# A hybrid decoder layer on one core: gate tiles of the delta rule end at slots 4 and 12, the recurrence's second gate products come one step later, and decode sums, loads and first tiles are moved

## What is computed

```python
def hybrid_layer(x, lw, dn_s0, dn_buf0, lru_h0, lru_buf0, mem_k, mem_v, fox_attend):
    h = rms_norm(x, lw['norm_w'])
    proj = jnp.einsum('bsd,de->bse', h, lw['w_in']) + lw['b_in']
    (dn_qkv, dn_z, dn_b, dn_a, lru_x, lru_g, fq, fk, fv, ff, fg, mq, mg, mgate) = jnp.split(proj, IN_OFFSETS, axis=-1)
    qkv, dn_buf = causal_conv(dn_qkv, dn_buf0, lw['dn_conv_w'])
    qkv = jax.nn.silu(qkv)
...
    o, dn_s = gated_delta_rule(q, k, v, beta, log_alpha, dn_s0)
...
...
    o = fox_attend(fq, fk, fv, logf)
    out_c = (o.reshape(bn, s, BR_WIDTH) * jax.nn.silu(fg)).astype(x.dtype)
...
    o = mem_attend(mq, mem_k, mem_v)
    out_m = (o.reshape(bn, s, BR_WIDTH) * jax.nn.silu(mg)).astype(x.dtype)
    branches = jnp.stack([out_a, out_b, out_c, out_m], axis=2)
    up = jnp.einsum('bsnw,nwd->bsnd', branches, lw['w_branch'])
    gates = jax.nn.sigmoid(mgate.reshape(bn, s, N_BRANCH, D_MODEL))
    merged = jnp.sum(gates * up, axis=2)
    y = x + jnp.einsum('bsd,de->bse', merged, lw['w_out'])
```

## Time and profile before

| | |
|---|---|
| median of 3 runs | 1766.01 us (1761.44 to 1767.62) |
| profiled execution | 1764.75 us, its span 1763.1 us |
| PE busy | 1677.8 us, 95% of the span |
| DVE busy | 789.7 us, 45% |
| ACT busy | 533.0 us, 30% |
| POOL busy | 513.8 us, 29% |
| DMA | 163.21 MB, mean 93 GB/s |

### The profile page before, as it was taken

How to read it: one execution, slowest core, us unless ns; L and a number is a source line. 1 busy time by engine, 2 the same in 40 slices (tenths; PEclk the granted TensorE clock), 3 DMA queues, 4 the chain that set the end, 5 groups by cost and what they waited for, 6 DMA issues and landing times. The chain is left out here.

```text
span 1763.1 us, 26818 instructions
## 1 busy us (share of the span) xinstructions
PE 1677.8 (95%) x11027; PEld 1603.1 (91%) x11027; DVE 789.7 (45%) x1200; ACT 533.0 (30%) x895; POOL 513.8 (29%) x387
## 2 busy tenths in 40 slices
PE   5999989999999999889999999999999989999999
PEld 5899989999999999889889898999989988899976
DVE  5485753333333334650365511344667431734611
ACT  6222343222222222233234323321145213544300
POOL 1343316333334314611344331112211211012300
PEclk9999999999999999999999999999999999999999
DMA  4211154222222116423365342145210322433531
GB/s 136 50 42 46 49 153 114 67 67 67 65 56 67 49 49 174 143 73 96 92 173 158 108 132 88 51 132 150 66 36 25 112 81 84 136 96 118 154 91 55
DMA packets 189366, 163.21 MB, mean 93 GB/s; under 512 B 18380, under 2 KB 157055, under 8 KB 188726
## 3 DMA queue, kind: packets, MB, share of 16 engines
q1 hardware_dynamic: 189246, 161.51, 31.7%
HBM read 131.38 MB, written 30.22 MB: 92 GB/s over the span
## 5 line engine op out<-in xcount | busy, mean ns | idle before, releaser
L275 POOL TENSOR_TENSOR wL<-w_raw,wH 128x1024 fp32r<-128x1024 f32 (+1 forms) x113 | 245.7, 2174 | 860.4 <-ACT wH L268 860.3
L299 PE MATMUL ps<-hH,wH 128*128 128x344 f32 x1920 | 448.1, 342 | 20.7 <-PEq L195 7.7
L299 PE MATMUL ps<-hL,wH 128*128 128x344 f32 x1920 | 410.2, 322 | 0.0
L299 PE MATMUL ps<-hH,wL 128*128 128x344 f32 x1920 | 409.1, 322 | 0.0
L299 PEld LDWEIGHTS ps<-hH,wH 128*128 128x128 f32 x1920 | 314.2, 191 | 34.1 <-issue 23.9
L299 PEld LDWEIGHTS ps<-hL,wH 128*128 128x128 f32 x1920 | 326.5, 190 | 0.0
L299 PEld LDWEIGHTS ps<-hH,wL 128*128 128x128 f32 x1920 | 324.3, 190 | 0.0
L268 ACT ACTIVATE wH<-w_raw 128x1024 fp32r<-128x1024 f32 (+1 forms) x116 | 108.4, 934 | 112.9 <-PE ps L299 96.1
L2776 POOL TENSOR_SCALAR fa_logits<-fox_c_bc,token_scalars 128x128 f32<-128x128 f32 (+7 forms) x32 | 56.3, 1758 | 68.7 <-PE ps L2801 50.5
L2919 DVE SCALAR_TENSOR_TENSOR fa_logits<-ps,fox_rq,fa_logits 128x512 f32<-128x512 f32 (+3 forms) x48 | 28.2, 613 | 106.8 <-POOL fa_logits L2777 56.8
L1757 ACT ACTIVATE d_m<-ps 128x512 f32<-128x512 f32 x48 | 28.6, 595 | 141.9 <-PE ps L1933 141.9
(11 more groups left out here) (560 smaller groups left out, 2820.5 us busy)
## 6 DMA issues: line engine op xcount, KB each, us to landing
w_raw<-in_w_in SPq DMA_DIRECT2D x80, 512.0 KB, 5.3
m_th<-gate_spill SPq DMA_DIRECT2D x28, 516.0 KB, 4.5
gate_spill<-d_gate SPq DMA_DIRECT2D x18, 516.0 KB, 3.0
fa_kv<-in_cache_fox_k SPq DMA_DIRECT2D x32, 256.0 KB, 3.1
fa_kv<-in_cache_fox_v SPq DMA_DIRECT2D x32, 256.0 KB, 3.2
w_raw<-in_w_branch SPq DMA_DIRECT2D x32, 256.0 KB, 2.7
gate_spill<-fa_gate SPq DMA_DIRECT2D x10, 516.0 KB
x_rows<-in_x_prompt SPq DMA_DIRECT2D x8, 512.0 KB, 6.2
```

Of the source, the lines that this page charges most:

```text
L275: pool.tensor_tensor(self.wL[:, t % 2, 0:nk], self.raw_at(t)[:, 0:nk], self.wH[:, t % 2, 0:nk].bitcast(F32), ALU.subtract).then_inc(self.w ...
L299: last = pe.matmul(self.ps[:, b + g, 0:cols], w[:, t % 2, k], x[:, k, g * cols:(g + 1) * cols], start=(k == 0 and n == 0), stop=(k == nk - ...
```

## The change

Parts, in the order of the program. Names are those of the diff.

- **A, setup.** x_sample is loaded first, weights 1 to 3 earlier. `first_tiles` (`two_tiles`) runs column group 0 (344 columns, from x rows 0 to 3) of tiles 0 and 1 first, while the second half of h is made, and then groups 1 and 2 of both. One of the nine row blocks is scaled on POOL. The small columns come two tiles later.
- **B, dn_z.** DVE splits the second memory tile's low part ahead of the last silu product, not after.
- **C, delta rule.** `FIRST = 11`: 11 steps of gate tiles run before chunk 0, so that tiles end at slots 4 and 12; ACT empties them at slots 5 and 13 and splits weights at 6 and 14. POOL's `identity` and the late weights' split come ahead of the Gram part of the chunk after.
- **D, fk.** The weights of tile end + 2 are loaded ahead of the eight stores of the decode states.
- **E and I, fq and mq.** `ahead` and `project_alone`: tile 0 of fq and of mq runs before the barrier, and the row turns beside these tiles come one tile later.
- **F, attend.** The sums of the decode values are made by DVE: a product in place over NP x 512, for fox a sum of halves, then a sum into QB or DLG; PE only adds over the partitions by one 128x1 matmul with ones, two iterations later. KEYS, VALUES and the softmax's places are tables, denser for fox and later for the memory. LEAD and NORMS are 6 and 4 for both.
- **G and L, after attend.** The last two turns of the output (`owed`) run ahead of steps 1 and 4 of the next tile.
- **H, lru.** `k -= j`: the products of tile j come j steps later, the tail at step 2 of tile 2.

```diff
-    def project_step(self, pe, t, xH, xL, k, groups=3, cols=G3):
+    def project_step(self, pe, t, xH, xL, k, groups=3, cols=G3, only=None):
...
+    def project_alone(self, t):
+        @self.block.tensor
+        def _(pe):
+            self.project(pe, t, self.hH, self.hL)
+    def project(self, pe, t, xH, xL, groups=3, cols=G3, meanwhile=None):
+        owed, self.owed = self.owed, {}
         for k in range(self.tiles[t][1]):
-            if ahead:
-                ahead(k)
+            if k in owed:
+                owed[k](pe)
...
+        def two_tiles(pe):
+            for k in range(KD):
+                pe.wait_ge(lo, k + 1)
+                K.project_step(pe, 0, K.hH, K.hL, k, only=(0,))
+                if k < 2:
+                    turn(pe, 6 + k)
+                if k == 4:
+                    pe.wait_ge(by_act, 1)
+                    pe.wait_ge(by_dve, 6)
+                    pe.wait_ge(by_pool, 1)
+                if k >= 4:
+                    turn(pe, 4 + k)
+            for k in range(KD):
+                K.project_step(pe, 1, K.hH, K.hL, k, only=(0,))
...
+            pe.wait_ge(sample, 3)
+            for k in range(KD):
+                pe.wait_ge(lo, KD + k + 1)
+                K.project_step(pe, 0, K.hH, K.hL, k, only=(1, 2))
+            for k in range(KD):
+                K.project_step(pe, 1, K.hH, K.hL, k, only=(1, 2))
...
+                    if j == 3 and next_by_dve:
+                        dve.wait_ge(K.w_lo, K.at_lo)
+                        K.split_lo(dve, t0 + 4 + 2)
...
+        FIRST = 11
...
+                        if s == 5:
+                            gate(mid(ch))
+                        if s == 13:
+                            gate(late(ch))
...
-                        bulk(tile_of(ch, s), s % 8)
+                        q = FIRST + SLOTS * ch + s
+                        bulk(t0 + q // KD, q % KD)
...
-        if (j, k) == (2, 0):
+        if (j, k) == (2, 2):
             pe.wait_ge(N["gate"], 24)
             self.tail.pe(pe, 0)
+        k -= j
...
                 if side:
+                    K.loads(sp, end + 3)
                     side.sync_last(sp)
...
-    LEAD, NORMS = (6, 4) if fox else (3, 2)
+    LEAD, NORMS = 6, 4
...
+    if fox:
+        KEYS, LOGF, MAX, EXP, TURN, LAST = (3, 4, 5, 6, 7, 11, 12, 13), 14, 15, 16, 17, 31
+        VALUES = (19, 20, 21, 22, 23, 27, 28, 29)
+    else:
+        KEYS, LOGF, MAX, EXP, TURN, LAST = (4, 6, 8, 10, 12, 14, 16, 18), 19, 19, 20, 21, 31
+        VALUES = (22, 23, 24, 25, 26, 27, 28, 29)
...
-                    for g in range(NP):
-                        last = pe.matmul(BANK[:, r:r + 1], KV[:, b % 2, g, h], PC[:, g, r:r + 1],
-                                         start=(g == 0), stop=(g == NP - 1))
+                    last = pe.matmul(BANK[:, r:r + 1], SUMS[b % 2][:, h], K.ones[:], start=True, stop=True)
...
-                turn_back(len(its) - 2)
-                turn_back(len(its) - 1)
+                K.owed = {1: lambda pe: turn_back(len(its) - 2), 4: lambda pe: turn_back(len(its) - 1)}
...
+                def decode_values(b):
...
+                    v.do(dve.tensor_tensor(kv, kv, PC[:, :, b * H:(b + 1) * H].unsqueeze(3).broadcast_to(
+                        [P, NP, H, P]), ALU.mult))
+                    if NP == 4:
+                        v.do(dve.tensor_tensor(kv[:, 0:2], kv[:, 0:2], kv[:, 2:4], ALU.add))
...
+                    dve.tensor_tensor(SUMS[b % 2], kv[:, 0], kv[:, 1], ALU.add).then_inc(M["vs"], 1)
```

More of the change, by code:

```diff
@@ L399, in _ @@
             act.wait_ge(filled, 1)
-            for t in range(9):
+            for x, t in enumerate((TT8, 0, 1, 2, 3, 4, 5, 6, 7)):
                 n = P if t < TT8 else NB
@@ L415, in _ @@
             act.activation(K.hH[:, :, SEQ:TOK], HS[:], ACT.Identity).then_inc(sample, 1)
-            for x in range(5, 10):
+            for x in range(11, len(TURNS)):
                 high(x)
-            K.split_hi(act, 2)
-            for x in range(10, len(TURNS)):
-                high(x)
+            K.split_hi(act, 3)
             act.wait_ge(tabT, 1)
@@ L471, in turn @@
             g, k = TURNS[x]
-            if x >= 5:
-                pe.wait_ge(lo, x - 4)
+            if held(x) is not None:
+                pe.wait_ge(lo, held(x) + 1)
             for y, t in enumerate(GROUPS[g]):
@@ L492, in _ @@
             pe.wait_ge(by_dve, 4)
[L493 to L501 removed]
+            for x in range(6):
                 turn(pe, x)
@@ L773, in _ @@
                                        bias=K.bias[:, b:b + 1]).then_inc(K.evac_act, 1)
-                    if small and j == 0:
+                    if small and j == 2:
                         small.act_split(act)
@@ L830, in _ @@
             def _(pe):
-                for j in range(n):
-                    if small and j == 3:
+                if first_tiles:
+                    first_tiles(pe)
+                for j in range(2 if first_tiles else 0, n):
+                    if small and j == 5:
                         pe.wait_ge(small.N["z"], 1)
                     K.project(pe, t0 + j, K.hH, K.hL,
-                              meanwhile=small and (lambda k, j=j: small.pe_step(pe, j, k)),
-                              ahead=ready and j == 0 and (lambda k: ready(pe, k)))
+                              meanwhile=small and (lambda k, j=j: small.pe_step(pe, j, k)))
                     if 3 <= j < squares + 3:
@@ L1094, in sync @@
                 each(sp, d)
-        K.loads(sp, self.end + 2)
+        K.loads(sp, self.end + (3 if self.ahead else 2))
         if self.fetch:
@@ L1182, in _ @@
             def _(pool):
-                m.pool(pool, m.end + 1)
+                m.pool(pool, m.end + (2 if m.ahead else 1))
             @block.scalar
@@ L1187, in _ @@
                 m.act(act, m.end + 1)
+                if m.ahead:
+                    K.split_hi(act, m.end + 2)
             @block.vector
@@ L2008, in _ @@
                         turn(0)
+                for q in range(KD, FIRST):
+                    bulk(t0 + q // KD, q % KD)
                 for ch in range(NCH):
@@ L2424, in _ @@
                 if side:
+                    K.loads(sp, end + 3)
                     side.sync_last(sp)
+                if ahead:
+                    K.loads(sp, end + 3)
                 if settle:
@@ L2441, in _ @@
                     K.split_lo(pool, end + 1 if preload else end)
+                if ahead:
+                    K.split_lo(pool, end + 2)
             @block.scalar
@@ L2470, in _ @@
                         act.activation(SQ[:, j % 2], DST[:, j, 0:SEQ], ACT.Square).then_inc(sq, 1)
+                if ahead:
+                    K.split_hi(act, end + 2)
                 if late:
@@ L2477, in _ @@
                     pe.wait_ge(*first)
-                for j in range(n):
+                for j in range(1 if begun else 0, n):
                     todo = of(j)
@@ L3209, in build @@
                 project_tiles(K, at["fv"], 4, BROW["fv"], VX, "fv", turns=turns,
-                              rows=(k_rows, sizes, K.knw, after), late=decode, ready=K.emptied(at["fv"] - 1), turned_first=True,
+                              rows=(k_rows, sizes, K.knw, after), late=decode, ready=K.emptied(at["fv"] - 1), turned_first=True, ahead=True,
                               stores=[((turns.normed, j + 1), d, k_rows[j])
                                       for j, d in enumerate(rows_of("fox_k", "fox_k_s"))])
+            K.project_alone(at["fq"])
         with K.joined():
@@ L3216, in build @@
             turns = RowTurns(K, "fvr")
-            after = [turns.out(j // 3, VX[:, :, cols(j)], v_rows[j], n) for j, n in enumerate(sizes)]
+            after = [turns.out(1 + j // 3, VX[:, :, cols(j)], v_rows[j], n) for j, n in enumerate(sizes)]
             c_in, pg_in = K.sem("fox_c_in"), K.sem("fox_pages_in")
-            project_tiles(K, at["fq"], 4, BROW["fq"], K.merged, "fq", turns=turns, RQ=RQ,
+            project_tiles(K, at["fq"], 4, BROW["fq"], K.merged, "fq", turns=turns, RQ=RQ, begun=True,
                           early=[(C[:].rearrange("p (t d) -> p t d", d=P),
@@ L3253, in build @@
             merge_branch(K, at["merge1"], 1, BranchIn(K, "m1", G, K.OT, K.OT_r), here[1],
-                         fetch=(KV, K.d_mkv, K.sem("mem_kv_in")), late=lru)
+                         fetch=(KV, K.d_mkv, K.sem("mem_kv_in")), late=lru, ahead=True)
+            K.project_alone(at["mq"])
         with K.joined():
@@ L3262, in build @@
             cols = lambda j: slice(j * P, (j + 1) * P)
-            after = [turns.out(0, KX[:, :, cols(j)], KR[:, j], P) for j in range(2)]
+            after = [turns.out(1, KX[:, :, cols(j)], KR[:, j], P) for j in range(2)]
             v_after = [turns.out(1, VX[:, :, cols(j)], VR[:, j], P) for j in range(2)]
```

224 lines of the change are left out of this document (119 added, 105 removed).

## The result

The changed kernel takes 1750.04 us (median of 6, 1746.49 to 1752.94) against 1764.08 for the kernel before in the same sessions: ratio 0.9923, 95% interval 0.9901 to 0.9945. One of the six runs of the kernel before took 5896.39 us; it is in the median and not in the ratio. The change is faster, as forecast, but by 14 us (0.8%) and not by 53; 1750 lies above the range. In the profiled execution the span is 1744.8 us against 1763.1.

What follows compares the result with a forecast made beforehand. The prediction took PE's work plus some 85 us of idle time as the bound (TensorE busy 1677.8 of 1763.1 us). Its terms summed to 53.2 us off 1764.75, forecast 1711.5 us, range 1695 to 1727.

Steps and rivals of the forecast that it cites:

- so if PE gets there 0.41 us sooner, PE waits 0.66 instead of 0.25: Delta rule: PE reaches slot 15 sooner but waits longer at slot 2 for DVE's chain; gain 0, bounds +3 and -7.
- rival 1: Delta chunks: POOL's early Gram part meets DVE's norm chain at slots 0 to 2; 7 us lost, 1718.5; chance 0.18.
- the prediction's own price: PE's timeline: a stretch of about 3.4 us at 0.55 clock costs 1.5 us on top of its gap.
- The prediction's own test: Delta rule, slot 2: PE's wait grows from 0.25 to about 0.66 us, or is 1.2 or more under rival 1.
- the sentence on no slack: Delta rule: argument for rival 1 that DVE's chain before PE's wait at slot 2 has no slack.
- no gap of 3 us before 60: Setup: sign expected in the profile after, with group 0 of tiles 0 and 1 ahead of the rest.
- Ahead of it the split waits only for its high part: First memory tile's neighbour: low part split ahead of the silu product; gain 2.2 us, bounds 0 and 2.67.
- the forecast give-back: fv: what PE gains at the first tile's wait it waits for at the row norms; D's term -1.5 us.
- the price of a record: Decode values on PE, fox and memory: 0.101 us per 128x1 product record; moving them to DVE gains 25.8 us.
- 14.5 busy in 100: Fox's attention: DVE busy 14.5 of 100 us, so its new sums were costed at nothing.
- rival 4: Both attentions: DVE becomes the bound, its 50.2 us of sums are paid, plus dips; 1786 us, chance 0.03.
- Rivals 2: Fox's keys in consecutive iterations stall on loads, 2.5 us in each of five; 12.5 us, 1724; chance 0.11.

Runs made afterwards that it cites:

- With POOL's wait: Changed kernel, with POOL's second part of a chunk's Gram work held until DVE has the norm of the last output: 1710.72 us, ratio 0.9699.

## Why the prediction was right and wrong

**Where it failed: part C.** The step reads "so if PE gets there 0.41 us sooner, PE waits 0.66 instead of 0.25. I take 0, bounds +3 and -7 (rival 1)". It cost 31.7 us alone. The step moved PE's arrival and kept the length of DVE's chain; the runs show that the chain itself grew. Rival 1 named the right engines and the right place, and the right start (POOL's first Gram part behind the late split), but it had that first part meet the norm chain. In the trace the first part meets the predicated copy ahead of the chain, and the operations that hold the chain are those of the second part. Its price was "One more in each of seven chunks goes straight into PE's wait", 1 us, and its chance 0.18. What the sum lacked is that a blocked operation delays the chain, and a delayed chain meets more POOL operations: 0.85 us at the start became five blocked operations where two had been, and 4.67 us of wait instead of 0.25. Behind the wait stands a dip of 3.5 us at 0.53, some 1.5 us by the prediction's own price. With the 45.00 us of the chunk without waits that is 45.00 + 4.67 + 1.5 = 51.17, measured 51.18. The prediction's own test separates them: "grows to about 0.66; under rival 1 it is 1.2 or more". It was 4.67. And the sentence on no slack should have set the bound: a chain of twelve small operations in front of PE, each able to wait out an operation of 1.0 to 1.3 us, is bounded by POOL's whole second part of 6.3 us (449.71 to 456.04), not by one operation. With the prediction's seven chunks that bound is some 44 us.

The Trainium skill (SBUF — State Buffer, sections Who interferes with whom and Summary: rules for kernel authors) states that a DVE instruction with two SBUF inputs contends with a GpSimd instruction that reads SBUF, and that the one that comes second fully blocks until the first finishes. The trace agrees to 0.02 us in the five ends above. The first of these sections of the Trainium skill also states that a reduction (tensor_reduce on trn2) never contends. The trace agrees: beside the chain's own reduction no POOL operation ran, but elsewhere one over 512 columns (719.68 to 720.37) took its usual 0.69 inside a POOL split of 718.98 to 721.91, and the product of 128x4 behind it then took 1.53. The prediction used that rule on the new sums and not on the chain, where it decided. On the new sums in fox the hold was small: one product of eight took 4.10 us where the median is 2.27, and the three groups together took some 3 us more than at their medians, not some tens.

**Part A** was 6.8 and gave 3.2. The two waits went, but the new one on hL is 3.63 us with a dip, not 1.3 in all, and the sign "no gap of 3 us before 60" did not come. Most of that wait is the same blocking: it fell to 1.54 in the run with POOL's wait in the setup.

**Part B** was 2.2 and gave 0.6: the wait of 2.67 at the second memory tile fell to 0.64, but the one ahead of the sixth grew from 0.88 to 2.74. The step "Ahead of it the split waits only for its high part" was right for one tile and left a later one uncosted. In both traces ACT has two exponentials ahead of the sixth tile's high part, and these wait for POOL's d_dT. PE comes there 5.6 us sooner than before and that POOL operation begins only 2.7 us sooner (263.45 against 266.17), so ACT's wait grew from 0.26 to 2.73. No run was made on it; this is read from the traces alone.

**Parts D and E** were 0 together and cost 3.9. E's barrier waits 1.95 as forecast. D was mis-sized at both ends. The first wait fell by 0.4, since ACT's first emptying there waits for the stores too (8.87 us, for out_dn_state_s). The second grew from 1.28 to 6.14. Some 2 us of that are the forecast give-back, as PE comes 2.1 us sooner after the stores have landed; another 2 us are one small operation of the norms, this time beside a POOL split of 784.16 to 786.50:

```profile
784.27 2.28 DVE L106 SCALAR_TENSOR_TENSOR fv_rn<-fv_tm,fv_rn 128x36 f32<-128x36 f32 x1
```

Its neighbours take 0.20. Undone, 3 us come back by the medians.

**Parts F, H, I to L were right.** F in fox gave 30.9 against 26.4 (24.9 in PE's busy time, 6.0 in its idle time); putting the products back costs 30.9 in the whole, against 25.8. So the price of a record was a little low: PE's busy time differs by 32.0 us for 256 records, 0.125 us each, where the rows of the products alone gave 0.101. What the products cost PE beside those rows was not tried. DVE's sums took 2.51, 1.33 and about 0.74 for fox, against 2.43, 1.23 and 0.69, and were hidden: over fox DVE went from 104 busy of 233 us to 140 of 202, and PE has no long wait for it. The "14.5 busy in 100" against rival 4 was read in a part of fox where DVE had little to do; that rival 4 would not come was right all the same. The barriers wait 1.95 and 1.66 (1.9 forecast), the recurrence 0.61 (0.6), the norms 1.63 (1.7), merge 3 5.16 for branch_in_r (4 to 5), which alone is a loss of 3.9.

**Rivals 2 and 4** did not come: no stall over 1.3 us in fox, DVE is not the bound. With POOL's wait the time is 1710.7, beside 1711.5 forecast; but that is luck in part: the other terms gave 47 of 53, and the repaired part C gave some 6 where the forecast had 0.
